# Other start addresses for the split weights, the token tiles and the hidden tiles of an expert feed-forward

## The reference, cut to what matters

```python
def expert_choice_ffn(h, router_w, w1, w3, w2):
    cap = EC_FACTOR * L // N_EXPERTS                     # 256 tokens for each of 16 experts
    aff = jax.nn.softmax(jnp.einsum('bld,de->ble', h, router_w).astype(jnp.float32), axis=-1)
    gate, idx = lax.top_k(jnp.swapaxes(aff, 1, 2), cap)
    xs = h[bidx, idx]
    hid = jax.nn.silu(jnp.einsum('becd,edf->becf', xs, w1)) * jnp.einsum('becd,edf->becf', xs, w3)
    y = jnp.einsum('becf,efd->becd', hid, w2) * gate[..., None].astype(h.dtype)
    return jnp.zeros_like(h).at[bidx, idx].add(y)
```

## The kernel before

| tiles | role | before, mod 1024 (mod 256) | after, mod 1024 (mod 256) |
|---|---|---|---|
| shi, slo | stationary in the up product, moving in the down product | 768 (0) | 32 (32) |
| xt_hi, xt_lo | moving in the up product | 800 (32) | 96 (96) |
| ht_hi, ht_lo | stationary in the down product | 0 (0) | 288 (32) |
| xs | gathered tokens | 768 (0) | 32 (32) |
| yo | result, scattered | 0 (0) | 288 (32) |
| fw, fjunk | final norm | 160 (160) | 448 (192) |
| spare | rows of the final norm | 544 (32) | 736 (224) |
| whi, wlo (not changed) | stationary in the projection | 512 (0) | 512 (0) |
| h_hi, h_lo, hc_hi, hc_lo (not changed) | moving in the projection, hc with 256 columns | 768 (0) | 768 (0) |
| wraw (not changed) | raw weights of the projection | 480 (224) | 480 (224) |
| xb (not changed) | token rows, and weights of the modulation, as loaded | 768 (0) | 768 (0) |

## Time and profile before

### The profile page before, as it was taken

The page is one execution under the profiler, slowest core; times in us unless marked ns, Lnnn a source line. Parts: engine busy times, 40 slices in busy tenths (PEclk is TensorE's granted clock), DMA queues, the critical chain, the costliest instruction groups (busy, mean ns, idle before and its releaser), DMA issues.

```text
span 2153.4 us, 35090 instructions
## 1 busy us (share of the span) xinstructions
PE 2074.0 (96%) x13569; PEld 1813.9 (84%) x13569; DVE 1370.2 (64%) x2082; ACT 996.3 (46%) x1630; POOL 278.0 (13%) x357
## 2 busy tenths in 40 slices
PE   6999999999999899997999999999999999999996
PEld 4778888888878677785999999999999999999985
DVE  3564548995994577757555656556555665656557
ACT  5923454444531445431444544445444444444455
POOL 0001100100001010020011112111221112111120
PEclk9999999999999999998999999999999999999998
DMA  7464333333327665456356666576565765657565
GB/s 258 150 240 136 112 107 99 114 113 94 125 76 237 235 209 178 144 213 257 118 207 243 218 217 208 190 259 214 196 218 191 273 203 186 216 214 258 196 230 225
DMA packets 188285, 407.95 MB, mean 189 GB/s; under 512 B 15956, under 2 KB 53396, under 8 KB 187300
## 3 DMA queue, kind: packets, MB, share of 16 engines
q1 hardware_dynamic: 162212, 318.36, 42.6%
q0 software_dynamic: 25984, 88.39, 12.6%
HBM read 329.59 MB, written 77.12 MB: 189 GB/s over the span
## 4 chain that ended last, share of the span: by engine, by line
PE 81%; DVE 10%; issue 3%; DMA 3%; ACT 2%; SPq 1%; POOL 0%; DVEq 0%; ACTq 0%; POOLq 0%
PE bh L55 11%; PE bh L57 11%; PE bh L56 11%; PE bank L55 8%; PE bank L57 8%; PE bank L56 8%; PE eby L55 5%; PE eby L57 5%; PE eby L56 5%; DVE acc L854 3%; PE ebt L2286 1%; PE bank L1037 1%; PE bank L1419 1%; DVE over L2018 1%; DVE raw L2474 1%
## 5 line engine op out<-in xcount | busy, mean ns | idle before, releaser
L55 PE MATMUL bh<-xt_hi,shi 128*128 128x256 f32 x2048 | 572.0, 279 | 3.0 <-DVE slo L2438 2.4
L56 PE MATMUL bh<-xt_lo,shi 128*128 128x256 f32 x2048 | 571.7, 279 | 0.0
L57 PE MATMUL bh<-xt_hi,slo 128*128 128x256 f32 x2048 | 571.7, 279 | 0.0
L2438 DVE TENSOR_TENSOR slo<-raw,shi 128x1024 fp32r<-128x1024 f32 x384 | 455.9, 1221 | 157.1 <-ACT shi L2348 153.0
L2348 ACT ACTIVATE shi<-raw 128x1024 fp32r<-128x1024 f32 x384 | 389.9, 1053 | 129.0 <-PE eby L57 127.2
L55 PEld LDWEIGHTS bh<-xt_hi,shi 128*128 128x128 f32 x2048 | 385.7, 188 | 4.2 <-issue 2.0
L56 PEld LDWEIGHTS bh<-xt_lo,shi 128*128 128x128 f32 x2048 | 385.8, 188 | 0.6
L57 PEld LDWEIGHTS bh<-xt_hi,slo 128*128 128x128 f32 x2048 | 385.8, 188 | 0.0
L55 PE MATMUL bank<-h_hi,whi 128*128 128x512 f32 x704 | 283.3, 402 | 0.0
L57 PE MATMUL bank<-h_hi,wlo 128*128 128x512 f32 x704 | 275.9, 392 | 0.0
L56 PE MATMUL bank<-h_lo,whi 128*128 128x512 f32 x704 | 275.7, 392 | 0.0
(11 more groups left out here) (347 smaller groups left out, 3121.7 us busy)
## 6 DMA issues: line engine op xcount, KB each, us to landing
raw<-in_exp_w_dram SPq DMA_DIRECT2D x96, 2048.0 KB, 11.1
uT<-stage POOLq DMA_DIRECT2D x72, 256.0 KB, 2.8
xb<-in_ada_w_dram SPq DMA_DIRECT2D x24, 512.0 KB, 6.0
wraw<-in_w_in_dram SPq DMA_DIRECT2D x22, 512.0 KB, 5.0
adaw<-in_ada_w_dram SPq DMA_DIRECT2D x8, 1024.0 KB, 10.1
xb<-in_x_dram SPq DMA_DIRECT2D x16, 512.0 KB, 4.4
xt<-in_x_dram POOLq DMA_DIRECT2D x16, 512.0 KB, 5.4
x2d<-xt POOLq DMA_DIRECT2D x16, 512.0 KB, 3.1
```

The source lines that it names most:

```text
L55: nc.tensor.matmul(out, w_hi, x_hi, start=start, stop=False)
L56: nc.tensor.matmul(out, w_hi, x_lo, start=False, stop=False)
L57: return nc.tensor.matmul(out, w_lo, x_hi, start=False, stop=stop)
L2438: nc.vector.tensor_tensor(item_dst(slo, n), item_src(n), item_dst(shi, n), ALU.subtract).then_inc(S["w_lo_ready"], 1)
```

## The change

Three things: the order and start addresses of the tiles in `phase_experts` (`behind(shift, unit)` moves the next tile up to the next address that is `shift` more than a multiple of `unit`); `shi` and `slo` now alternate, so `shi3` begins at 146464 and not at 133888; and ACT waits for `list_ready` ahead of the fourth split of expert 0. Four small tiles of the final norm become slices of one, which takes fewer padding bytes. No instruction is added, removed or put elsewhere on any engine, apart from that one wait; loads and stores have the same sizes.

```diff
@@ route_stage
         v.hot_free = (S["blocks_ready"], 1)
+        v.found_free = (S["list_ready"], 1)
@@ phase_experts
         raw, raw_loaded = v.raw, v.s_raw
-        shi = [sb(f"shi{i}", [P, D], F32R) for i in range(NR)]
-        slo = [sb(f"slo{i}", [P, D], F32R) for i in range(NR)]
+
+        def behind(shift, unit):
+            at[0] += (shift - at[0]) % unit
+
+        behind(32, 1024)
+        shi, slo = [], []
+        for i in range(NR):
+            shi.append(sb(f"shi{i}", [P, D], F32R))
+            slo.append(sb(f"slo{i}", [P, D], F32R))
         xs_words = [sb(f"xs{i}", [P, D], F32R) for i in range(2)]
         xs = [t[:, :].bitcast(F32) for t in xs_words]
-        at[0] += 32
+        behind(96, 1024)
         xt_hi, xt_lo = sb("xt_hi", [P, KD, CAP], F32R), sb("xt_lo", [P, KD, CAP], F32R)
-        at[0] += 224
+        behind(32, 256)
         ht_hi, ht_lo = sb("ht_hi", [P, FD, CAP], F32R), sb("ht_lo", [P, FD, CAP], F32R)
@@
-        ssq, msq, rst, nt = (sb("f_" + n, [P, NT + 2]) for n in ("ssq", "msq", "rst", "nt"))
+        small = sb("f_small", [P, 4 * (NT + 2)])
+        ssq, msq, rst, nt = (small[:, i * (NT + 2):(i + 1) * (NT + 2)] for i in range(4))
@@ ACT, ahead of the first expert
                 act.wait_ge(*v.hot_free)
                 for n in range(NR):
+                    if n == NR - 1:
+                        act.wait_ge(*v.found_free)
                     split(0, n)
```

## The result

The changed kernel takes 2160.86 us (median of 7 runs, 2158.75 to 2163.16) against 2153.88 us before (7 runs): a ratio of 1.0029, 95% interval 1.0019 to 1.0039. It is slower; I had forecast 2135.5 us. Two runs further on, one of b1 (3431.66 us) and one of the kernel before beside it (5909.92 us), are left out of the ratios and stand in the medians.

A forecast was written before the change was run, and what follows sets the result against it. PE's matmul pitch in experts 0 to 14 was taken as the bound. Up product 19.2 us less, all other terms 0: 2155.14 - 19.2 = 2135.9, on the median 2154.73 - 19.2 = 2135.5 us; range 2104 to 2157.

The forecast's parts named there:

- What bounds the kernel: Experts 0 to 14: time is a count of matmuls times their pitch, 67.9 of 68.07 us for an expert.
- Up product: the failed step: Up matmuls of experts 0 to 14: 64 apart takes 3.33 ns off each, pitch 113.3 ns, 19.2 us less.
- Down product: Down matmuls of experts 0 to 14: still no distance between the streams, 0 taken, bounds 4.8 us either way.
- Expert 15: Last expert: waits and the final norm take up a shorter pitch; 0 counted, at most 1.3 us more gain.
- the edits at nothing: Split writes of ACT and DVE at other addresses, and the turns of tokens with xs moved by 32: 0 taken.
- the wait: ACT's fourth split in expert 0: list done 1.5 us before ACT comes; 0 taken, uncovered at most 0.98 us.
- the transfers: Gathered and scattered rows now 32 behind a multiple of 256: 0 taken; the skill's rule gives 0.3 us.
- Slower: Rival, chance 0.17: every up matmul of experts 0 to 14 loses 3.33 ns, 19.2 us more, 2173.9 us.
- The larger gain: Rival, chance 0.22: up and down products both gain, constants 3.3 and 6.7 ns, 48 us less, 2107 us.
- the prediction's 59 us: Up and down products of 15 experts: estimate of what could still go by the skill's issue gap.

The follow-up runs named there:

- b1: Kernel before with xt at 192 behind a multiple of 256 instead of 32, ht still at 0: 2159.69 us, ratio 1.0023.
- d1: Kernel before with xt at 192, ht at 0 and only the fourth buffer pair (shi3, slo3) 128 bytes further: 2137.04 us, ratio 0.9926.
- the map: Three runs with each of the four shi/slo buffers at another address, so four distances per run: 2168.71, 2164.47 and 2173.53 us against 2155.2.
- c4: Kernel before with two transposes ahead of the up product in experts 1 to 15, no address changed: 2163.22 us, ratio 1.0040.
- a1: Changed kernel with xt at 64 behind 1024 instead of 96, so 32 bytes ahead of the weights again: 2154.57 us, ratio 0.9996.
- m5: Four buffers at 0, 256, 128 and 384 behind 512, xt at 192: 2142.69 us in one run against 2155.11 for the kernel before.
- d5: Changed kernel with xt at 224 (192 ahead of the weights) and the fourth buffer pair 128 bytes further: 2137.18 us, ratio 0.9919.
- d4: Kernel before with xt at 192 and slo3 alone 128 bytes further, shi3 at 0: 2140.92 us, ratio 0.9935.

## Why the prediction was wrong

*What bounds the kernel.* Right: PE's pitch in experts 0 to 14, with nothing else in the way. Each change of pitch came through in full, 0.40 us for an expert in the changed kernel and 1.16 in d1.

*Up product: the failed step.* It said: "Going from 0 to 32 apart took 3.3 ns off; I take one more such step for 64 apart, a constant of 6.7, pitch 113.3 ns." The runs show in its place that the constant is no ladder in the distance (0, 32, 64, 96: 119.8, 116.7, 117.8, 120.0 in the map), and not a function of the distance alone. At 32 it was 116.7 or 117.8 ns (before, c4; two experts of a1), at 192 113.3 or 117.8 (two experts of b1), at 64 117.8 or, carried in, 113.3 (m5). The changed kernel sits at 117.8, 1.1 ns above its old state. That 113.3 ns turned up after all, but elsewhere, says nothing for the step. Rows 3 and 4, from which I took the slope, differ in distance, in neighbours and in entry; I read the first alone.

*Down product.* 0, as predicted. But the ground was thin: I took the equal constants at distance 0 (13.3 ns for 256 and for 512 columns) as one number for both shapes. At 64 it is 11.1 for the up product and about 16 for the down product (229.3 less 213.3); at 32 it is 10.0 and 20.

*Expert 15, the edits at nothing, the wait, the transfers.* Right. For the edits, the wait and the transfers that is shown by a1, which has them all and costs nothing, and by the rows of the seam. Expert 15 has no run of its own; in d1 the other 15 experts' 15 x 1.16 = 17.4 us leave 0.2 of the 17.65 between the medians for it. In the profiled execution expert 15, from its first up to its last down matmul, was 1.1 us shorter than before, and the seam came 1.5 us earlier, neither tied to the change by a run; so that execution is 3.6 us longer while the medians differ by more.

*The rivals.* "Slower" had the place and the sign, with a size three times too large: 1.1 ns for a matmul, not 3.33, so 6.2 us (the ratio's 0.29%) and not 19.2. "SBUF — State Buffer" of the Trainium skill (Who interferes with whom) says that PE's two read ports are independent and that PE never waits on anyone. Taken as a rule by which start addresses do nothing to PE, as the prediction took it, a1 does not agree: the start of one tile, moved by 32 bytes, is worth 6 us and nothing else changed. Whether PE waits at a port, no run shows. The larger gain needed both products to gain; the steady pitch of the down product has not been below 226.7 ns in any run. "TensorE: Matmul & The Clock Gate" of the Trainium skill (Back-to-back issue gap) gives its columns / 2.4 plus 2.5 ns for an isolated matmul, so the prediction's 59 us were no measure of this stream; no run had a steady up pitch below 113.3 ns.

*Still open:* what gives 272, 280 and 282.7 cycles of 2.4 GHz as resting points (113.3, 116.7, 117.8 ns); which accesses meet, and whether the other one is PE's own (ACT and DVE write the split weights during the up product; that the pitch is the same in every item, while they are busy 32 and 41 of 68 us, speaks against them, but no run takes them away); what in an entry decides, since the same pause led to different pitches at one distance (a1 and before, d5 and d1); whether expert 0 settles alike in every execution, as each run left one trace; and whether distances finer than 32 bytes matter, as tiles here begin at multiples of 32.

## What to carry to other kernels

In a stream of fp32r matmuls that PE alone bounds, measure the pitch from start times, stage by stage and also for the first and the later passes of a loop: two passes over the same tiles may differ by 4%. Treat the start addresses as something to map and then to time in the whole kernel, since what stands ahead of the stream has a say in which of its pitches it settles at. A mean over items at several distances does not carry over to a kernel with one distance: the map's 114.4 ns at 192 became 117.8 in b1. Here the layout to use is d1's (0.9926 of the time before, 0.9919 in d5's layout): moving tile 192 ahead in the up product, 0 in the down product, and one buffer of four off by 128 bytes, with which experts 1 to 14 of both d1 and d5 run at 113.3 ns all through.

## What the runs showed of the hardware that I had not expected

One stream of matmuls on unmoved tiles has several steady pitches, exact to 0.01 ns from expert to expert: 113.33 and 117.78 ns at distance 192, 116.67 and 117.78 at 32. Two transposes ahead of 384 matmuls, which hold them up by some 0.2 us, are enough to change it for all of them (c4), and one displaced buffer in their midst changes it from there on (d4). Behind a pause of the same length it is not the same in each layout: 113.3 ns in expert 0 of d1 and 117.8 in that of d5, both at 192. The down product settles at only one pitch at distance 0, 226.7 ns, in every run, and at 229 to 235 at the others.
